# Moving state tails, channel means and part splits to other places in a hybrid trunk layer's projection stage

## What is computed

```
h = rmsnorm(x, g_mix[l])
z = jnp.einsum('btd,de->bte', h, w_in[l])
a_b, a_c, a_x, p_x, c_a, c_g, d_u, d_v = jnp.split(z, 8, axis=-1)
y_a, sa = causal_dwconv(a_c * a_x, st_a[l], conv_a_w[l])       # 3 taps
y_a = a_b * y_a
y_p, sp = multiscale_pool(p_x, st_p[l], pool_w[l], pool_scale[l], start_pos)
y_c, sc = causal_dwconv(c_a * jax.nn.sigmoid(c_g), st_c[l], conv_c_w[l])   # 31 taps
y_c = jax.nn.silu(layernorm(y_c + conv_c_b[l], ln_c_g[l], ln_c_b[l]))
v_n = layernorm(d_v, ln_d_g[l], ln_d_b[l])
y_d = d_u * chunk_spatial_mix(v_n, sgu_w[l], sgu_b[l])
mix = jnp.concatenate([y_a, y_p, y_c, y_d], axis=-1)
x = x + jnp.einsum('bte,ed->btd', mix, w_out[l])
h = rmsnorm(x, g_ffn[l])
x = x + hier_moe(h, ...)        # top group of 4, top 2 of its 8 experts
```

## Time and profile before

| | us |
|---|---|
| median of 3 runs | 673.23 |
| runs | 671.88 to 674.0 |
| profiled execution, its time | 673.23 |
| profiled execution, its span | 671.4 |
| PE busy | 580.5 (86%) |
| DVE busy | 369.5 (55%) |
| ACT busy | 204.3 (30%) |

### The profile page before, as it was taken

One profiled execution on the slowest core, in us unless ns is written; L12 is line 12 of the kernel. 1 busy time (PEld: TensorE's weight loads), 2 busy tenths in 40 slices (PEclk: granted clock), 3 DMA queues, 4 the chain that ended last, 5 costly groups with the idle time before them and its releaser, 6 DMA issues. The chain is left out here.

```text
span 671.4 us, 9514 instructions
## 1 busy us (share of the span) xinstructions
PE 580.5 (86%) x3131; PEld 496.4 (74%) x3131; DVE 369.5 (55%) x653; ACT 204.3 (30%) x351; POOL 97.6 (15%) x151
## 2 busy tenths in 40 slices
PE   3899999999999998999999449999999999997000
PEld 2899999988898897888887338777778777774000
DVE  4838997999996966566665841111111111112497
ACT  6732112311324273122121123233333323332132
POOL 4300002000000000000000231332233333322000
PEclk9999999999999999999999759999999999999555
DMA  9660211120122123641220776888989999940784
GB/s 320 133 143 1 63 32 32 53 63 16 48 72 95 33 94 138 238 157 64 95 79 32 255 241 218 297 307 285 317 294 351 367 316 344 322 186 26 288 349 161
DMA packets 51439, 116.27 MB, mean 173 GB/s; under 512 B 8434, under 2 KB 26743, under 8 KB 50295
## 3 DMA queue, kind: packets, MB, share of 16 engines
q1 hardware_dynamic: 42899, 92.82, 40.7%
q0 software_dynamic: 6656, 17.84, 7.6%
q10 hardware_dynamic: 1828, 4.96, 2.0%
HBM read 99.75 MB, written 20.68 MB: 179 GB/s over the span
## 5 line engine op out<-in xcount | busy, mean ns | idle before, releaser
L1663 PE MATMUL ps<-at_hT,at_ring 128*128 128x384 f32 x936 | 165.7, 333 | 1.1 <-ACT at_wk L629 1.1
L1663 PEld LDWEIGHTS ps<-at_hT,at_ring 128*128 128x128 f32 x936 | 155.8, 188 | 6.5 <-issue 5.0
L1840 PE MATMUL ps<-at_hT,at_mring 128*128 128x512 f32 (+1 forms) x432 | 102.6, 393 | 1.9 <-DVE at_mring L1343 1.2
L1840 PEld LDWEIGHTS ps<-at_hT,at_mring 128*128 128x128 f32 (+1 forms) x432 | 77.3, 182 | 21.2 <-DVE at_mring L1343 1.6
L1542 DVE TENSOR_TENSOR at_actv<-at_sg,ps 128x128 f32<-128x128 f32 x35 | 10.1, 287 | 146.2 <-ACT at_sg L869 101.6
L1190 DVE SCALAR_TENSOR_TENSOR at_mixP<-at_uc,sb_par,at_mixP 128x1024 f32<-128x1024 f32 x60 | 77.4, 1289 | 2.1
L1932 PE MATMUL ps<-at_wlater,at_hTm 128*128 128x256 f32 x320 | 72.4, 379 | 0.0
L1932 PEld LDWEIGHTS ps<-at_wlater,at_hTm 128*128 128x128 f32 x320 | 59.2, 190 | 7.2
L1932 PE MATMUL ps<-at_wfirst,at_hTm 128*128 128x256 f32 x240 | 56.3, 389 | 0.0
L1918 PEld LDWEIGHTS ps<-sb_ident,at_xg 128*128 128x128 f32 x280 | 37.7, 193 | 23.6 <-issue 21.8
L1932 PEld LDWEIGHTS ps<-at_wfirst,at_hTm 128*128 128x128 f32 x240 | 45.9, 197 | 6.3 <-issue 0.3
(11 more groups left out here) (238 smaller groups left out, 656.4 us busy)
## 6 DMA issues: line engine op xcount, KB each, us to landing
at_wlater<-in_expert_w_gate SPq DMA_DIRECT2D x20, 512.0 KB
at_wlater<-in_expert_w_up SPq DMA_DIRECT2D x20, 512.0 KB
at_wlater<-in_expert_w_down SPq DMA_DIRECT2D x20, 512.0 KB
at_raw<-in_w_in SPq DMA_DIRECT2D x16, 512.0 KB, 4.0
at_opair_p<-scratch_out SPq DMA_DIRECT2D x8, 1024.0 KB, 12.0
at_wfirst<-in_expert_w_gate SPq DMA_DIRECT2D x15, 512.0 KB
at_wfirst<-in_expert_w_up SPq DMA_DIRECT2D x15, 512.0 KB
at_wfirst<-in_expert_w_down SPq DMA_DIRECT2D x15, 512.0 KB
```

What stands on the lines that cost most here:

```text
L1663: mm = pe.matmul(ps[:, bank + r, 0:t1 - t0], w[:, wpart, k * P:(k + 1) * P], hT[:, hpart, k, t0:t1], start=(m, wpart, hpart) == (0, 0, 0), ...
L1840: mm = pe.matmul(ps[0:n, b + r, :], mring[:, 1 - i % 2, mpart, k * P:k * P + n], wo[:, wpart, k, r * 512:(r + 1) * 512], start=(c, mpart, ...
```

## The change

Nothing is computed in another way; instructions of four queues stand in another order.

- PE: the pooling tails move from behind m = 2 of ac0 to behind m = 0, the pool products from m = 4, 5, 6 to 2, 3, 4. The means move from m = 1, 2, 3 of ax1 to 2, 4, 6. The tails of mixer A's half 0 move from ax1 to ab0 (m = 0), the variances from m = 0, 1, 2 of ab0 to 2, 3, 4, and the tails of half 1 from ab0 to ab1 (m = 4).
- DVE: the pooling of half 1 stands six taps earlier, all taps and `sample_c(1)` stand before `part_lo(13)` and `a_input(0)`, and all eight parts of `w_out` are split before `a_gate(1)`; the first mixture columns are split before the second part.
- ACT: the squares stand before the first tail copy, the Silus before the tails of half 1 are stored, and all parts of `w_out` before `mix_hi_first(0, 2)`.

```diff
@@ ACT @@
-            act.wait_ge(s["ua_ready"], 1)
-            tail_copy(wk[:, 0, :], HA, HA)
             for r in range(3):
                 ln_square(r)
...
+            act.wait_ge(s["ua_ready"], 1)
+            tail_copy(wk[:, 0, :], HA, HA)
             part_hi(15)
             act.wait_ge(s["stage_out"], stages[0])
             a_state_part(0)
...
             tail_copy(wk[:, 1, :], HA, HA)
+
+            for c in range(2):
+                act.wait_ge(s["c_norm"], 1)
+                for y in mix_parts(4 + c):
+                    do(A(y, y, ACT.Silu, bias=par[:, c, 37:38], scale=par[:, c, 36:37]), s["c_ready"])
             a_state_part(1)
             act.dma_start(a["new_conv_a_prompt"][0, 0], stage[0:HA, 0, :]).then_inc(s["stage_out"], 16)
...
-            act.wait_ge(s["v_out"], 16)
-            act.wait_ge(s["conv_ready"], 1)
-            for c in range(2):
-                act.wait_ge(s["c_norm"], 1)
-                for y in mix_parts(4 + c):
-                    do(A(y, y, ACT.Silu, bias=par[:, c, 37:38], scale=par[:, c, 36:37]), s["c_ready"])
...
             part_hi(NPIECE)
+            act.wait_ge(s["v_out"], 16)
+            act.wait_ge(s["conv_ready"], 1)
             mix_hi_first(2, KC, "mixa_hi")
-            for c in range(1, 6):
+            for c in range(1, KC):
                 part_hi(NPIECE + c)
             act.wait_ge(s["mix_first"], 1)
             mix_hi_first(0, 2, "mh_hi")
-            for c in range(6, KC):
-                part_hi(NPIECE + c)
@@ DVE @@
             spatial(LAST)
+            part_lo(11)
+            taps_c(1, 16, 20)
+            part_lo(12)
+            pool_means(1, pool_sums(1))
+            taps_c(1, 20, 31)
+            sample_c(1)
+            do(v.tensor_copy(sc[:, 7:8], ones[:, 0:1]), s["conv_ready"])
+            part_lo(13)
...
-            part_lo(11)
-            taps_c(1, 16, 22)
-            part_lo(12)
-            taps_c(1, 22, 26)
-            pool_means(1, pool_sums(1))
-            taps_c(1, 26, 31)
-            part_lo(13)
             a_input(0, 11)
-            sample_c(1)
-            do(v.tensor_copy(sc[:, 7:8], ones[:, 0:1]), s["conv_ready"])
             a_taps(0)
...
             part_lo(NPIECE)
-            part_lo(NPIECE + 1)
             mix_lo_first(2, KC, "mixa_hi", "mixa_lo")
-            for c in range(2, 5):
+            for c in range(1, KC):
                 part_lo(NPIECE + c)
             a_gate(1, 15)
-            for c in range(5, KC):
-                part_lo(NPIECE + c)
@@ PE @@
             def behind_ac0(m):
-                if m == 2:
+                if m == 0:
                     pe.wait_ge(s["px_ready"], 1)
                     tails("pst0", wk[:, 0, :], HP, HP)
-                if m in (4, 5, 6):
-                    pool_product(0, m - 4)
+                if m in (2, 3, 4):
+                    pool_product(0, m - 2)
...
             def behind_ax1(m):
-                if m in (1, 2, 3):
-                    r = m - 1
+                if m in (2, 4, 6):
+                    r = m // 2 - 1
                     pe.wait_ge(s["conv_ready"], 1)
                     over_channels("mean", r, mix_cols(4, 6, r))
-                if m == 5:
+            def behind_ab0(m):
+
+                if m == 0:
                     pe.wait_ge(s["ua_ready"], 1)
                     tails("ast0", wk[:, 0, :], HA, HA)
-            def behind_ab0(m):
-
-                if m in (0, 1, 2):
-                    r = m
+                if m in (2, 3, 4):
+                    r = m - 2
                     pe.wait_ge(s["c_sq"], r + 1)
                     over_channels("var", r, ln_cols(lnsq2[:] if r == 2 else lnsq[:, r, :, :], r))
-                if m == 6:
+            def behind_ab1(m):
+
+                if m == 4:
                     pe.wait_ge(s["ua_ready"], 2)
                     tails("ast1", wk[:, 1, :], HA, HA)
...
-            z(15, order=WO)
+            z(15, order=WO, behind=behind_ab1)
```

## The result

The changed kernel takes 685.2 us in the median (684.4 to 685.7); the kernel before, 673.5 us beside it. The ratio is 1.0174 (95% interval 1.0153 to 1.0194), +11.7 us. The forecast was 680.4 us with a range up to 684. The direction held; the size did not.

The account below looks back on a forecast made before the run. PE was taken to bound the kernel until the routing tail, with DVE a close second. The steps' delays, partly inside one another, came to +7.2 us: span 671.4 + 7.2 = 678.6, plus 1.83 above span, 680.4 us; range 677 to 684.

Parts of the forecast that it names:

- What bounds the kernel: Until the routing tail PE bounds: a microsecond of PE waiting added between 160 and 260 us lengthens the span by one.
- Step 1: Pooling tails two groups earlier in ac0: PE waits 3.1 us for ACT's sptmp copy; ax0 starts 2.0 us later.
- Step 2: DVE's order before a_input(0): DVE loses 3.5 us at the earlier pooling; ax1 starts 5.0 us late, step 1's 2.0 included.
- Steps 3 and 4: Later pieces, mixer C's norm, ACT's order: ab0 +5.2 us, ab1's end +5.4, first w_out copy 7.7 later; PE waits 0.2.
- Step 5: Output projection of tile 0: PE waits 2.5 us for mh_lo 1; project(1) at 266.6 instead of 259.40, +7.2 us.
- Rival (a): TensorE's clock falls in a new wait, slowing matmuls 2.0 us each time: 682.4 for one, 684.4 for both; chance 0.11.
- (b): DVE doesn't wait at the pooling or catches up, so ax1 waits for nothing: near +3.8, 677.0 us; chance 0.08.
- (c): The delay is swallowed by PE's idle stretch from 374 us on: not slower, about 673 us; chance 0.06.

Follow-up runs that it names:

- ac0 alone: The kernel before with only the change's ac0 part (pooling tails behind m = 0, products behind 2, 3, 4): 677.0 us, ratio 1.0059.
- idle time alone: The kernel before, with PE waiting once in ac1 for small memsets on GpSimd: 677.7 us with 17 memsets, 676.3 us with 10.
- the filled kernel: The changed kernel with matmuls of no use filling most of PE's waits in ac0, ahead of ax1 and in project(0): 682.0 us, ratio 1.0126.

## Why the prediction was wrong, step by step

**What bounds the kernel: right.** PE waiting that was added in this stage came back in the time, also where no other engine was late (ac0 alone, idle time alone), and less only where it lay inside a later wait, as the first did inside the second.

**Step 1, the wait in ac0: right, its price incomplete.** Forecast 3.1 us, with the first transpose counted in; the trace has 2.66 behind that transpose. The step's sentence that "they and ACT's work behind them keep their time" failed: the products came at 170.51 instead of 167.9, because eighteen matmuls ran at 1.2 GHz.

**Step 2, DVE ahead of a_input(0): right.** DVE's timeline of the changed kernel:

```profile
178.54 4.36 DVE L1281 TENSOR_TENSOR at_wk<-at_wk 128x1222 f32<-128x1222 f32 x3 [6.40 <-ACT sb_acts L741]
...
186.68 14.49 DVE L1189 SCALAR_TENSOR_TENSOR at_mixP<-at_uc,sb_par,at_mixP 128x1024 f32<-128x1024 f32 x11
...
207.84 1.42 DVE L1334 TENSOR_TENSOR at_wk<-ps,at_mixP 128x768 f32<-128x768 f32 x2
```

DVE stands for ACT's marker as said, 6.40 us instead of 3.5 because the marker is late by the first fall. With the waits filled it is 3.69 us from 172.6 to 176.31, and ax1 starts at 207.44 where I had 206.7. In that execution everything was 0.6 us late already at the start of ac0 (160.53 instead of 159.95), so the step is right to 0.2 us.

**Steps 3 and 4: right to some tenths.** With the waits filled: ab0 at 223.88 (forecast 223.0), project(0) at 252.78 (forecast 251.8); less the 0.6 they are 0.3 and 0.4 late. The early Silus and the later means, variances and tails are a cost of their own, 2.1 us, shown by the kernel that has only them.

**Step 5, project(0): right, 0.3 us too short.** The wait for mh_lo 1 is 3.09 us, forecast 2.5. I had taken the low end, 0.2 us, for the load of the last w_out parts. With the waits filled, ACT stands 1.68 and 0.22 us for these loads, and DVE then 0.57 us for ACT:

```profile
258.38 1.06 ACT L606 ACTIVATE at_hT<-at_wo_m 128x1024 fp32r<-128x1024 f32 x1 [1.68 <-DMA at_wo_m<-in_w_out]
259.66 1.06 ACT L606 ACTIVATE at_hT<-at_wo_m 128x1024 fp32r<-128x1024 f32 x1 [0.22 <-DMA at_wo_m<-in_w_out]
...
259.55 2.50 DVE L1149 TENSOR_TENSOR at_hT<-at_wo_m,at_hT 128x1024 fp32r<-128x1024 f32 x2 [0.57 <-ACT at_hT L606]
```

In all, project(1) stands 8.5 us later than in the earlier trace rows (267.88 against 259.40), 7.9 without the late start; the forecast was 7.2. The filled kernel is 8.5 (ratio) to 9.0 us (medians) above before. The 0.6 to 1.1 us between 7.9 and that are spread behind project(1) and over the noise of single executions; I can't assign them to a cause.

**Rival (a): this is the step that failed.** The sum put the clock at nothing. I had two rows, 1.1 us of idle time without a fall and 4.40 us with one, called the new waits of 3 us nearer to the longer, and still gave a fall 0.11 and took the reading that there is none. Nothing in the rows was a reason for that. Between the two rows the outcome was open, and a range that covered all three falls would have ended near 686. The runs show that 1.95 us can be enough, and what the falls cost on the median is 3.2 us (685.2 less 682.0); in the profiled execution, with all three, 6.5.

The Trainium skill ("TensorE: Matmul & The Clock Gate", section "Loop structure matters more than you think") says that PE goes cold in a long DMA wait between matmuls, 8 us in its example, and that the matmul behind it runs cold. That this covers waits of 3 us was the prediction's reading of it; so read it gave 686, nearer than the sum. The trace of the changed kernel agrees with that reading in all three places; the 2.38 and 2.75 us waits of two of the experiments had no fall.

The sum of the waits was short as well, by 1.3 to 1.8 us (7.2 forecast, 8.5 to 9.0 measured). Neither error alone takes the time out of the range: 680.4 + 3.2 is 683.6, and the filled kernel has 682.0. Together they do.

**Rivals (b) and (c): did not happen.** Ax1 waited 3.29 us. The idle stretch after 374 us took up nothing: the same three waits of 6.4, 4.4 and 3.5 us stand in it as before (6.2, 4.4 and 3.5).

The 11.7 us, then: some 8.5 of waits (7.2 forecast) and some 3.2 of lower clock (none forecast).

## What to carry to other kernels

When the bounding engine is TensorE, cost a new wait twice: the wait itself, and the matmuls behind it at half rate, which here, where the clock fell, came to between 1.3 and 2.7 us a time for waits of 2 to 5 us; if the only bounds on that are far apart, the range has to hold both. Moving a step earlier in an in-order queue buys nothing until its input is earlier too: ask who sets that input, and what stands behind the step. And look at the filler of the second engine (here the taps) as the buffer that it is: moving six taps behind a step turned them into 3.5 us of waiting and took the slack from everything after.

## What the hardware showed that I had not expected

Idle times of PE inside dense work, and what the granted clock did in the profiled execution: 1.1 to 1.2 us, never a fall; 1.95 us, a fall; 2.38 us, none, and 2.37 us in another kernel, one; 2.66 us, a fall in all four kernels that have this wait; 2.75 us, none, and 2.82 us, one; 3.1 to 3.3 us and 4.96 us, a fall each time. The clock went down about 2 us after PE had stopped in the first place of the change, and stayed at 1.2 GHz for some 7 us, of which PE worked the last 6. In the third place it went down only when PE was at work again, 3.9 us after it had stopped, and stayed down about half as long; there the matmuls lost 1.4 us instead of 2.5. In these runs neither whether a wait of 2 to 3 us brought a fall nor what the fall cost could be told from the length of the wait. Matmuls whose results nobody reads, put into the wait, kept it at 2.4 GHz and made the kernel 3.2 us faster.
